# Attention mask, query norm and row maximum in one VectorE instruction; norms kept as columns and spread by matmuls; the first five jobs on banks of their own

## The reference

```python
def rms_norm(x, w):                       # over the last axis
    return x * lax.rsqrt(jnp.mean(x * x, axis=-1, keepdims=True) + EPS) * w
...
    q = rms_norm(q.reshape(B, T, N_HEADS, HEAD_DIM), q_norm_w)      # 16 heads of 64
    k = rms_norm(k.reshape(B, T, N_KV_HEADS, HEAD_DIM), k_norm_w)   # 4 heads of 64
    ik = rms_norm(ik, idx_k_norm_w)
...
        score = jnp.where(visible, score, -jnp.inf)
        _, idx = lax.top_k(score, top_k)                            # 128 of up to 512 keys
...
        s = jnp.einsum('bqgrd,bqkgd->bqgrk', qg, k_sel).astype(jnp.float32) * scale
        s = jnp.where(valid[:, :, None, None, :], s, -jnp.inf)
        p = jax.nn.softmax(s, axis=-1).astype(v.dtype)
        o = jnp.einsum('bqgrk,bqkgd->bqgrd', p, v_sel)
```

## Time and profile before

| | |
|---|---|
| time, median of 3 runs | 1786.38 us (1783.95 to 1786.85) |
| the profiled execution, time | 1784.85 us |
| its span in the trace | 1783.1 us |
| TensorE busy | 1698.7 us (95%) |
| VectorE / ScalarE / GpSimd busy | 732.8 / 699.1 / 790.4 us |
| chain that ended last | PE 89%, DVE 5%, ACT 3%, issue 2% |
| TensorE's longest waits in total | 11.1 us (gates, for VectorE), 11.0 us (first head), 10.8 us (window attention), 10.5 us (start) |

### The profile page before, as it was taken

One profiled execution on the slowest core, in us unless ns is written; L12 is line 12 of the kernel. 1 busy time (PEld: TensorE's weight loads), 2 busy tenths in 40 slices (PEclk: granted clock), 3 DMA queues, 4 the chain that ended last, 5 costly groups with the idle time before them and its releaser, 6 DMA issues.

```text
span 1783.1 us, 23396 instructions
## 1 busy us (share of the span) xinstructions
PE 1698.7 (95%) x7710; PEld 1356.5 (76%) x7710; DVE 732.8 (41%) x1293; ACT 699.1 (39%) x1133; POOL 790.4 (44%) x1061
## 2 busy tenths in 40 slices
PE   5999996999999999999999999889999999999997
PEld 4686663667688888888888788578886888888885
DVE  5486688444423321212123342533312364253354
ACT  4421565444432342323234332754344443243242
POOL 5243453222245545554555353025662466565553
PEclk8998998999999999999999999889999999999998
DMA  4121121111132223232223222013331223223231
GB/s 168 61 83 65 54 88 53 36 47 48 42 124 94 95 94 102 89 104 94 95 93 106 81 95 83 1 36 118 118 130 36 83 94 107 91 97 106 89 100 59
DMA packets 45147, 149.79 MB, mean 84 GB/s; under 512 B 4664, under 2 KB 7872, under 8 KB 45088
## 3 DMA queue, kind: packets, MB, share of 16 engines
q1 hardware_dynamic: 38016, 138.43, 23.3%
...
## 4 chain that ended last, share of the span: by engine, by line
PE 89%; DVE 5%; ACT 3%; issue 2%; ACTq 0%; DVEq 0%
PE job L309 25%; PE job L311 25%; PE job L310 25%; PE o L501 2%; PE score L465 2%; DVE arena L1327 2%; PE turn L351 1%; PE score L398 1%; PE score L438 1%; DVE arena L1330 1%; DVE arena L1514 1%; PE job L754 1%; PE score L722 1%; PE job L692 1%; PE o L339 1%
## 5 line engine op out<-in xcount | busy, mean ns | idle before, releaser
L277 POOL TENSOR_TENSOR w_lo<-w_raw,w_hi 128x256 fp32r<-128x256 f32 x1056 | 789.7, 780 | 964.3 <-ACT w_hi L801 963.5
L309 PE MATMUL job<-a_hi,w_hi 128*128 128x512 f32 (+1 forms) x1144 | 446.0, 390 | 16.1 <-POOL w_lo L277 10.5
L310 PE MATMUL job<-a_lo,w_hi 128*128 128x512 f32 (+1 forms) x1144 | 435.0, 380 | 0.0
L311 PE MATMUL job<-a_hi,w_lo 128*128 128x512 f32 (+1 forms) x1144 | 434.9, 380 | 0.0
L801 ACT ACTIVATE w_hi<-w_raw 128x1024 fp32r<-128x1024 f32 x264 | 275.3, 1050 | 292.0 <-PE job L311 288.8
L309 PE MATMUL job<-b_hi,w_hi 128*128 128x512 f32 x952 | 377.9, 397 | 0.0
L311 PE MATMUL job<-b_hi,w_lo 128*128 128x512 f32 x952 | 371.0, 390 | 0.0
L310 PE MATMUL job<-b_lo,w_hi 128*128 128x512 f32 x952 | 370.5, 389 | 0.0
L309 PEld LDWEIGHTS job<-a_hi,w_hi 128*128 128x128 f32 x1144 | 217.7, 190 | 63.7 <-DVE a_lo L1327 10.7
L310 PEld LDWEIGHTS job<-a_lo,w_hi 128*128 128x128 f32 x1144 | 217.5, 190 | 41.7 <-issue 2.5
L311 PEld LDWEIGHTS job<-a_hi,w_lo 128*128 128x128 f32 x1144 | 217.2, 190 | 40.7
...
## 6 DMA issues: line engine op xcount, KB each, us to landing
w_raw<-w_all SPq DMA_DIRECT2D x264, 512.0 KB, 3.2
...
```

The costliest lines, as they stand in the source:

```text
L277: nc.gpsimd.tensor_tensor(w_lo[:, sl, c], raw[:, sl, c], w_hi[:, sl, c].bitcast(F32), ALU.subtract).then_inc(s("lo_ready"), 1)
L309: mm(ps[:, 0:n], w_hi[:, sl, c], hi[:, kt, 0:n], start=kt == 0, stop=False)
L310: mm(ps[:, 0:n], w_hi[:, sl, c], lo[:, kt, 0:n], start=False, stop=False)
L311: ins = mm(ps[:, 0:n], w_lo[:, sl, c], hi[:, kt, 0:n], start=False, stop=kt == last)
```

## The change

- **Start.** Jobs 2, 3 and 4 write to the three score banks, so the first five jobs need not wait for a take. Job 1 (`J_IQ`) runs in front of the first norm sum; the norm is inside job 2.
- **Norms as columns.** ACT takes the root straight from PSUM (`Sqrt` with scale 1/D and bias epsilon) into a column `rcol`, VectorE the reciprocal. The spread is four matmuls whose stationary operand is that column broadcast to 128 columns and whose moving operand is the identity. `rbuf`, `sel`, `row`, `turn_stat`, `rows` and the bf16 identity are gone. The spread stands after slice 4 of the job.
- **Keys.** Their sums stand in front of `J_Q`, their spreads (four matmuls for each of four heads, 64 rows each) behind it. The weight of the query norm is multiplied into the keys (`kqn`). VectorE takes `J_Q` before its first selection round and scales the keys in the first two pauses.
- **Queries.** No query tile is scaled. Their reciprocal norms stay as columns `rq`, negated.
- **Attention.** One VectorE instruction, `tensor_tensor_reduce`, reads the scores from PSUM and the mask from SBUF, adds them with the query norm as scale, writes the (negated) result to `prob` in SBUF, and reduces it by minimum to `nmax`. ACT's exponential reads SBUF with scale -1. The tile order is 3, 2, 1, 0, tiles 1 and 0 share a bank, and all four stand in front of the job. VectorE's 16 heads are written out, no loop.
- **Gated linear attention.** The sums of squares go between the outputs, the squares are taken from PSUM, and two spreads stand in front of the turn of v. The transfer `s_toep` is issued behind the split of job `J_IN2 + 21`.

The norm and the start, on TensorE:

```diff
-                sl, ps = k % SLOTS, job_ps[k % 2]
+                sl, ps = k % SLOTS, bank(k)
...
-                if not (isinstance(m, int) and k + 4 * m < 2):
-                    pe.wait_ge(s("job_taken"), 4 * m + (k - 1))
+                if not (isinstance(m, int) and k + 4 * m < 5):
+                    pe.wait_ge(s("job_taken"), 4 * m + (k - 1) if k > 6 else 2)
...
-            def norm_spread(c, k=None, hi=None, lo=None, n=T):
...
+            def spread(ps, col, tokens=QT, rows=slice(0, P)):
+
+                for t in range(tokens):
+                    ins = mm(ps[rows, t * P:t * P + P],
+                             rcol[:, t, col:col + 1].to_broadcast([P, rows.stop - rows.start]),
+                             ident, start=True, stop=True)
+                return ins
+
+            def norm_job(n, k, hi, lo, width=T, tokens=QT):
+
+                open_job(k)
+                block_of(k, range(0, 5), hi, lo, width, 7, early(k, 0))
+                pe.wait_ge(s("norm_inv"), n)
+                spread(t_ps[0], 0, tokens).then_inc(s("norm_spread"), 1)
+                block_of(k, range(5, 8), hi, lo, width, 7, early(k, 0)).then_inc(s("job_done"), 1)
...
-            norm_stat(0, 0)
-            norm_spread(0, J_IQ, a_hi, a_lo)
-            job(J_IQ + 1, a_hi, a_lo)
+            job(J_IQ, a_hi, a_lo)
+            pe.wait_ge(s("const_landed"), 16)
+            norm_sum(0)
+            norm_job(1, J_IQ + 1, a_hi, a_lo)
```

Keys and queries on TensorE, and VectorE's order there:

```diff
-            pe.wait_ge(s("qk_sq"), 2)
-            sum_stat(sq[:, 1], 0, halves).then_inc(s("qk_sum"), 1)
...
+            for c in range(2):
+                pe.wait_ge(s("qk_sq"), c + 2)
+                sum_stat(sq[:, 1 - c], 16 + 2 * c, halves).then_inc(s("qk_sum"), 1)
+            job(J_Q, a_hi, a_lo)
...
+            for c in range(2):
+                spread(t_ps[c], 4 + 2 * c, rows=slice(0, 64))
+                spread(t_ps[c], 5 + 2 * c, rows=slice(64, 128)).then_inc(s("qk_spread"), 1)
+            for k in range(8):
+                job(J_Q + k + 1, a_hi, a_lo)
...
-            for n in range(10):
-                if n >= 4:
-                    pe.wait_ge(s("qk_normed"), n - 3)
-                spread(n, (t_ps + s_ps)[n % 4][:]).then_inc(s("qk_spread"), 1)
...
+            dve.wait_ge(s("qk_root"), 2)
+            v.reciprocal(rcol[:, :, 4:8], rcol[:, :, 4:8]).then_inc(s("qk_inv"), 1)
+            dve.wait_ge(s("kv_zeroed"), 2)
+
+            take(J_Q, p1[:, J_Q, :])
             for c in range(8):
...
-                take(J_Q + c, p1[:, J_Q + c, :])
+                if c < 7:
+                    take(J_Q + c + 1, p1[:, J_Q + c + 1, :])
+                if c < 2:
+                    dve.wait_ge(s("qk_spread"), c + 2)
...
-            for n in range(10):
-                dve.wait_ge(s("qk_spread"), n + 2)
...
-                    stt(q, q, vcol("qn"), ps[:]).then_inc(s("qk_normed"), 1)
```

A head on TensorE and on VectorE:

```diff
-                    mm(ps[:, 0:w], identb[:], keep[:, qt, 0:w], start=True, stop=False)
-                    mm(ps[:, 0:w], q_now[:, u, qt * P:qt * P + P], kz[:, 2 * kvt + half, 0:w],
-                       start=False, stop=True).then_inc(s("att_mm"), 1)
+                    mm(ps, q_now[:, u, qt * P:qt * P + P], kz[:, 2 * kvt + half, 0:w],
+                       start=True, stop=True).then_inc(s("att_mm"), 1)
...
+                for e, qt in enumerate(ATT_ORDER):
+                    w = P * (qt + 1)
+                    dve.wait_ge(s("att_mm"), first + (4 if e == 2 else e + 1))
+                    v.tensor_tensor_reduce(prob[:, qt, 0:w], score_of(qt), keep[:, qt, 0:w], rq[:, qt, i * 4 + n:i * 4 + n + 1],
+                                           3.0e38, ALU.add, ALU.min, nmax[:, qt:qt + 1]).then_inc(s("att_max"), 1)
+                for e, qt in enumerate(ATT_ORDER):
+                    w = P * (qt + 1)
+                    dve.wait_ge(s("att_exp"), first + e + 1)
+                    did(v.reciprocal(rinv[:, qt:qt + 1], rsum[:, qt:qt + 1]))
+                    settle()
+                    ts(prob[:, qt, 0:w], prob[:, qt, 0:w], rinv[:, qt:qt + 1]).then_inc(s("att_prob"), 1)
```

407 lines of the change are left out of this document (169 added, 238 removed).

## The result

The changed kernel takes 1743.62 us (median of 4, 1742.31 to 1743.7), the kernel before beside it 1785.19 (1783.95 to 1786.85): a ratio of 0.9765, 95% interval 0.9749 to 0.978. The forecast was 1752, the range began at 1744. The sign was right, and so was what bounds the kernel; the gain of 41.6 us was underrated: the sum said 34.

The account below looks back on a forecast made before the run. TensorE's list and waits were taken to bound the kernel. Gains 7 + 13 + 1.5 + 9.6 + 3 + 2 - 2 = 34 us, from 1784.85 to 1750.8, as a median 1752; range 1744 to 1764.

Parts of the forecast that it names:

- What bounds the kernel: Whole kernel: TensorE, busy 95% of the span; a microsecond off its list or its waits is worth a microsecond.
- The start: Up to the index scores: job 1 fills the wait for the norm sum, a new 4 us stop follows; gain 7.
- Query jobs: From T, end of job `J_V + 1`, to `J_RNN + 2`: spreads go, VectorE sets the end; gain 13, with slow start.
- First head and heads: Attention: first head gains 1.5 us; 16 heads gain 0.6 each from mask matmuls and one cut fewer, 9.6.
- VectorE in the head: Four new instructions take 2.5 us, first tile ready at 4.3, wanted at 4.95 us; slack 0.65, nothing waits.
- Rival (a): Heads: new instruction as slow as the scan, heads lose 2.4 us instead of gaining 9.6; 1764 us, chance 0.12.
- Norms: Norm jobs: one break and eight passes replace turn and spread; gain 0.6 us each, five times: 3.
- The end: Last norm: ACT's copy, the turn and the wait between fall away; gain 2 us.
- Gated attention: Three sums move ahead of the last job, 2.8 us later; scores 9.5 us behind it; net loss 2.
- (b): Heads: new instruction still slower, the four over 5.25 us, so the kernel is slower than before; 1812 us, chance 0.04.
- (c): Start: the wait only turns into one for the reciprocal, lower clock into jobs 3 and 4; 1758 us, chance 0.10.
- (d): Gated part doesn't lose, query part gains 15 us, heads 0.75 each; 1744 us, chance 0.08.

Follow-up runs that it names:

- e1_select_first: Changed kernel, but VectorE starts the selection before it takes `J_Q`, key products one round pair later: 1738.66 us.
- e9_forms: Changed kernel with a tail of VectorE instructions on 128x512, alone and beside GpSimd; its rows count, not its time: new instruction alone 0.75 us.
- e5_four_pieces: Changed kernel, but each head's job cut into four parts instead of three, one slice between the turns of tiles 3 and 2: 1745.2 us.
- e14_late_turn: Changed kernel, but the turn of tile 2 stands between the last two slices of a head's job, as in the kernel before: 1751.63 us.
- e15_lone_small: Changed kernel, but the score of tile 0 alone stands behind the first slice of each head's job: 1744.15 us.
- e8_spreads_back: Changed kernel, but the first two spreads of the gated norm stand behind the first tile's window scores again: 1745.22 us.
- e11_sums_behind: Changed kernel, but all four gated-norm sums stand behind job `J_IN2 + 18`, and ACT takes the roots after them: 1749.77 us.

## Why the prediction was right or wrong

**What bounds the kernel** was right: TensorE's list and its waits. The gains could be read as waits or matmuls of TensorE, save where the clock wanders.

**The start**, 7 forecast, 9.5 and (second pair) 8.0 measured. The steps hold: sum at 25.3, a new stop that ends at 33, no wait for VectorE's takes. The step "a new stop of 4 us, and I assume the lower clock behind it for 4 us" is one of two outcomes: in the second profile (stop 3.1, 4.4 us at 0.52, index scores 63.1 against the forecast 62.7) it is what happened, in the first one, as in nine of the 13 profiles with this start, it didn't. I treated as fixed a term that changes between executions. ("12 matmuls at twice 0.226 us cost 2.4 us extra" should be 2.7; nothing hangs on it.)

**Query jobs**, 13 forecast, 10.3 measured, the one term that was too high. VectorE bounds this part up to the end of the selection, as said: it ended at T + 67.7 (forecast 68.3). The failed step is "Masks and reciprocal on VectorE let `J_RNN + 2` begin at T + 70.9", with masks priced from the rows of before: the cast and three writes took 3.3 us in place of 1.05, as they had moved beside GpSimd's subtractions (`e1_select_first` and `e9_forms`). TensorE began at T + 72.4. And "the slow start 1.5 to 2.0" wasn't saved, since a wait of 2.8 us stood in its place: the next matmuls started 0.43 us apart again.

**First head and heads**, 11.1 forecast, 14.5 and 13.4 measured: the largest part of the miss. The failed step is "0.6 to 0.65 of 11.77 us per head": it measured 0.86. The mask matmuls in it are 0.56 against 0.55. "cut into three parts, not four, about 0.1 us each" failed: a cut is free (`e5_four_pieces`). What I put at nothing is that in the kernel before TensorE waits for ACT's copy of the late turn in front of every product with v: 0.27 per head with its restart, 4 us in all (`e14_late_turn`). It stood in the trace, as starts 0.46 or 0.35 us behind the last matmul where 0.23 is the rule, but each is too short to rise in the list of waits, and I read that list from the top. The first head gave 1.6 us in one pair of profiles and 0.3 in the other, against 1.5.

**VectorE in the head**: quartet 1.97 us against 2.5, tile 3 ready 3.7 us after the head's start, wanted at 4.9. Rival (a) rested on the scan's row. Alone, the new instruction takes 0.75 us whatever it reads. The Trainium skill, "Vector Engine (DVE) Microarchitecture Reference", "Points that are easy to get wrong", says of the form `S2S2D2_STT` that two sources in SBUF that aren't bf16 halve its rate. I carried that over to this instruction, which the page doesn't name. The row of two f32 tiles (0.75 us, 1745.99) shows no half rate here, so the time that I gave to scores copied to SBUF wouldn't have come by that rule; no run here tests the form that the page names.

**Norms**, 3 forecast, about 4 measured: job `J_FF + 1` takes 6.49 us from its first matmul to the next job's, before 7.39. With their slow restarts turn and spread of before took 0.44 and 1.25, 0.08 more than my 1.6, and the new spread 0.89, 0.1 less than mine; another 0.1 is one more restart in the last slices of before. The stages of three norms gave 1.0 each (the one above, and 43.8 to 42.8 and 359.0 to 358.1 from sum to sum behind it); the memory's gave nothing, since its stage, with the cross attention, kept its 136 us. The end: 2 forecast, 2.0 measured.

**Gated attention**, -2 forecast; the stage with its norm job gained 2.1 or 3.9. The sums in front of the job cost 2.7 (forecast 2.8), and the first window scores came 8.5 us behind it (forecast 9.5). The step "I make the scores 9.5 us after the job. Net loss 2" stopped the count there: two spreads that had stood behind that mark stood in front of it now. `J_OUT2` comes 64.7 us behind the job, before 70.2. Not all of that is the edit's. Windows from the first window scores to `J_OUT2` (columns as above): the kernel before, the changed kernel, and `e15_lone_small`, whose code in this part is the changed kernel's:

```profile
1120.45:1180.60 60.15, 45.72 (x242) 37.76 (x240) 30.34 (x74) 43.59 (x129) 0.00 (x0) 0.83 0.00 1
```

```profile
1085.06:1141.28 56.22, 38.27 (x249) 34.12 (x248) 30.29 (x74) 43.51 (x129) 0.00 (x0) 0.94 0.00 1
```

```profile
1089.91:1149.92 60.01, 42.23 (x250) 37.41 (x248) 30.28 (x74) 43.57 (x129) 0.00 (x0) 0.86 0.00 1
```

With the same code this part took 56.2 us at a granted clock of 0.94 and 60.0 at 0.86; four of the 15 profiles with this code have 60.0. The whole stage took from 241.7 to 247.2 us in these 15, 243.7 in the mean, and 245.6 in both profiles of the kernel before: a gain of 1.9 in the mean, 1.0 of it without the norm job, and a loss in one execution. `e8_spreads_back` shows that the place of the spreads makes no difference to the end; `e11_sums_behind` shows that the new arrangement without its early sums and squares is 5.9 us slower. What in the edit makes up for the 2.7 us, beside the clock, stays open.

**The rivals.** (a) and (b) fell with the row of 751 ns. (c) is half of the start's truth: the stop came, the lower clock sometimes, but in neither profile of the changed kernel into job 3. (d), 1744 at a chance of 0.08, named two of the right places (heads 0.75, a gated part without loss) and a wrong one (query 15). Its own terms add up to 40.4: 1744.5 against the profiled execution, but 1746 as a median, in which the other rivals are given. That the range reached down to 1744, 0.4 us from the result, comes from this slip and not from foresight.

So start, heads, norms and gated part were too small and the query part too large: 34 became 41.5 between the first two profiles. Of these only the heads' term is steady, with a cause that experiments show; start, first head and gated part move by 1.3 to 5.5 us between executions of the same code. The range took its width from one term at a time, and had no room for four small errors on the same side.
